# A list scheduler by highest level in place of one by program order, in a hybrid encoder block

## The reference

```python
h = rms_norm(x, norm_mix_g); proj = h @ w_in            # q 512, k 128, v 128, u 512
attn = window_attention(rope(q), rope(k), v, sink)      # 128-token blocks, +-128 window
ys = s5_bidirectional(u, ...)                           # 32 groups, complex state of 64,
                                                        # one scan in each direction
ys = gelu(ys); ys = ys * sigmoid(ys @ w_glu)
mixed = concat(rms_norm(attn), rms_norm(ys)); x = x + mixed @ w_out
h = rms_norm(x, norm_ffn_g)
up = depthwise_conv(h @ w_up, conv_w, conv_b)           # width 3, 2 x 2816 channels
x = x + (silu(up[gate]) * up[val]) @ w_down
return rms_norm(x, norm_final_g)
```

## Time and profile before

| | before |
|---|---|
| median of 3 runs | 1464.31 us (1461.26 to 1465.69) |
| profiled execution | 1461.61 us, span of the slowest core 1460.1 us |
| spans of the 8 cores | 1448.3 to 1460.1 us |
| PE, DVE, ACT busy | 1068.9, 989.2, 810.6 us |
| chain that ended last | PE 52%, DVE 17%, issue 12%, DMA 9%, ACT 8% |
| activation table loads | 20, of 1283 ns |

### The profile page before, as it was taken

How to read it: one execution, slowest core, us unless ns; L and a number is a source line. 1 busy time by engine, 2 the same in 40 slices (tenths; PEclk the granted TensorE clock), 3 DMA queues, 4 the chain that set the end, 5 groups by cost and what they waited for, 6 DMA issues and landing times.

```text
span 1460.1 us, 22892 instructions; the slowest of 8 cores (1448.3 to 1460.1 us)
## 1 busy us (share of the span) xinstructions
PE 1068.9 (73%) x6969; PEld 543.3 (37%) x6969; DVE 989.2 (68%) x1780; ACT 810.6 (56%) x1543; POOL 47.5 (3%) x63
## 2 busy tenths in 40 slices
PE   0159883686558577520887887599999999869996
PEld 0125441474323122110444444244544444424442
DVE  1576764848998999930677777388888888814322
ACT  2565562774333533252777776298888888723111
POOL 0001001010001000000000000000000000000000
PEclk9979987685555555555788888799999999979998
DMA  6743330000000000322122222522222221085331
GB/s 160 211 126 116 100 115 17 1 1 1 1 1 1 0 0 0 95 87 86 38 80 88 69 76 88 145 62 85 59 86 61 73 73 30 1 280 205 107 116 72
DMA packets 71320, 109.97 MB, mean 75 GB/s; under 512 B 4544, under 2 KB 50368, under 8 KB 71072
## 3 DMA queue, kind: packets, MB, share of 16 engines
q1 hardware_dynamic: 65344, 87.66, 20.7%
q0 software_dynamic: 5856, 20.85, 3.6%
HBM read 87.65 MB, written 20.85 MB: 74 GB/s over the span
## 4 chain that ended last, share of the span: by engine, by line
PE 52%; DVE 17%; issue 12%; DMA 9%; ACT 8%; SPq 1%; POOL 1%; DVEq 0%; ACTq 0%; POOLq 0%
PE ps L362 48%; DVE sb L342 11%; ACT sb L338 8%; PE ps L370 3%; DMA sb<-w_down 2%; DVE sb L787 2%; DVE sb L789 2%; DMA sb<-w_out 2%; DVE sb L354 1%; DMA sb<-x 1%; DVE sb L876 1%; DMA sb<-w_in 1%; PE ps L816 1%; DMA sb<-w_glu 1%; DMA sb<-w_up 1%
## 5 line engine op out<-in xcount | busy, mean ns | idle before, releaser
L362 PE MATMUL ps<-sb,sb 128*128 128x512 bf16 (+6 forms) x5089 | 779.6, 308 | 153.0 <-ACT sb L338 90.3
L362 PEld LDWEIGHTS ps<-sb,sb 128*128 128x128 bf16 (+1 forms) x5089 | 392.0, 101 | 535.5 <-issue 224.2
L338 ACT ACTIVATE sb<-sb 128x1 f32<-128x1 f32 (+11 forms) x589 | 340.4, 592 | 394.3 <-DVE sb L342 234.2
L338 ACT ACTIVATE sb<-ps 128x512 f32<-128x512 f32 (+7 forms) x666 | 323.0, 500 | 175.2 <-PE ps L362 142.7
L354 DVE SCALAR_TENSOR_TENSOR sb<-sb,sb,sb 128x1024 f32<-128x1024 f32 (+3 forms) x275 | 332.8, 1216 | 48.0 <-ACT sb L338 36.5
L342 DVE TENSOR_TENSOR sb<-sb,sb 128x272 f32<-128x272 bf16 (+10 forms) x572 | 287.7, 531 | 97.7 <-ACT sb L338 75.7
L342 DVE TENSOR_TENSOR sb<-ps,sb 128x512 f32<-128x512 f32 (+4 forms) x372 | 176.7, 498 | 103.4 <-PE ps L362 77.5
L769 PE MATMUL ps<-sb,sb 32*128 32x272 bf16 (+1 forms) x512 | 158.0, 509 | 72.2 <-DVE sb L342 72.2
L370 PE MATMUL ps<-sb,sb 128*128 128x128 bf16 x724 | 73.7, 269 | 100.6 <-DVE sb L342 55.3
L769 PEld LDWEIGHTS ps<-sb,sb 32*128 32x128 bf16 x512 | 64.4, 134 | 164.8 <-issue 146.8
L338 ACT ACTIVATE sb<-sb,sb,sb 128x1024 f32<-128x1024 f32 x88 | 109.2, 1241 | 5.1
(11 more groups left out here) (35 smaller groups left out, 154.2 us busy)
## 6 DMA issues: line engine op xcount, KB each, us to landing
sb<-x SPq DMA_DIRECT2D x49, 512.0 KB, 4.5
sb<-w_up SPq DMA_DIRECT2D x44, 512.0 KB, 3.9
sb<-w_down SPq DMA_DIRECT2D x22, 512.0 KB, 5.7
x_scr<-sb POOLq DMA_DIRECT2D x17, 512.0 KB, 5.1
sb<-x_scr SPq DMA_DIRECT2D x16, 512.0 KB, 3.7
y<-sb POOLq DMA_DIRECT2D x16, 512.0 KB, 2.9
sb<-w_in SPq DMA_DIRECT2D x8, 640.0 KB, 6.4
sb<-w_out SPq DMA_DIRECT2D x8, 512.0 KB, 3.8
```

What stands on the lines that cost most here:

```text
L338: return e.activation(out=out, in_=in_, func=func, scale=scale, **kw)
L362: ins = e.matmul(out, l, r, start=(i == 0), stop=(i == n - 1))
```

## The change

A second planner, `schedule_hlf`, is added and used (`KS_MODE` has 1 as its default; with 0 the old one is used). It first computes for each operation its level `bl`: its own planned cost and the largest level among its successors with a hop of 0.45 us, barriers included. Then it goes forward in time: of all engines it takes the one that can start something first; there, all operations that are ready by then are moved to a heap ordered by falling level (program order only breaks ties), and the highest is placed. Nothing else is changed: the operations, tiles, costs, predecessors and the way in which waits are written stay. Small differences: an operation without predecessors is ready at 0 instead of 0.45 us, and a barrier adds no hop of its own.

```diff
--- before.py
+++ after.py
@@ -159,9 +159,79 @@
         assert all(o.start is not None for o in ops), "scheduler: unscheduled ops (cycle?)"
         self.makespan = max(o.end for o in ops)
 
+    def schedule_hlf(self):
+        import heapq
+        ops = self.ops
+        succ = {id(o): [] for o in ops}
+        for o in ops:
+            for p in o.preds:
+                succ[id(p)].append(o)
+        bl = {}
+        for o in reversed(ops):
+            m = 0.0
+            for s_ in succ[id(o)]:
+                v = bl[id(s_)] + self.HOP
+                if v > m:
+                    m = v
+            bl[id(o)] = o.cost + m
+        npred = {id(o): len(o.preds) for o in ops}
+        eng_of = lambda o: self.streams[o.stream].eng_name
+        eng_free = {e: 0.0 for e in self.ENGS}
+        cand = {e: [] for e in self.ENGS}
+        avail = {e: [] for e in self.ENGS}
+
+        def rtime(o):
+            return (max(p.end for p in o.preds) + self.HOP) if o.preds else 0.0
+
+        def release(o):
+            for s_ in succ[id(o)]:
+                npred[id(s_)] -= 1
+                if npred[id(s_)] == 0:
+                    add(s_)
+
+        def add(o):
+            if o.stream is None:
+                o.start = o.end = max([p.end for p in o.preds], default=0.0)
+                release(o)
+            else:
+                heapq.heappush(cand[eng_of(o)], (rtime(o), o.prog, o))
+        for o in ops:
+            if npred[id(o)] == 0:
+                add(o)
+        left = sum(1 for o in ops if o.stream is not None)
+        while left:
+            best_e, best_t = None, None
+            for e in self.ENGS:
+                while cand[e] and cand[e][0][0] <= eng_free[e] + 1e-9:
+                    rt, pg, o = heapq.heappop(cand[e])
+                    heapq.heappush(avail[e], (-bl[id(o)], pg, o))
+                if avail[e]:
+                    t_ = eng_free[e]
+                elif cand[e]:
+                    t_ = max(eng_free[e], cand[e][0][0])
+                else:
+                    continue
+                if best_t is None or t_ < best_t:
+                    best_e, best_t = e, t_
+            e = best_e
+            if not avail[e]:
+                eng_free[e] = best_t
+                continue
+            _, pg, o = heapq.heappop(avail[e])
+            o.start = best_t
+            is_dma = self.streams[o.stream].inc == 16
+            o.end = best_t + o.cost
+            eng_free[e] = best_t + (0.08 if is_dma else o.cost)
+            left -= 1
+            release(o)
+        assert all(o.start is not None for o in ops)
+
     def emit(self, block):
         self.barrier()
-        self.schedule()
+        if _C("KS_MODE", 1) >= 1:
+            self.schedule_hlf()
+        else:
+            self.schedule()
         per_eng = {e: [] for e in self.ENGS}
         for o in self.ops:
             if o.stream is not None:
```

## The result

| | before | after |
|---|---|---|
| median | 1463.53 us (12 runs) | 1452.94 us (12 runs) |
| ratio | 1 | 0.9937, 95% interval 0.992 to 0.9953 |
| profiled execution | 1461.61 us | 1454.08 us |

Faster by 0.6%, where I had forecast 1.9% (1437 us). The sign and the range held, the size did not: of 27 us, about a third came.

What follows compares the result with a forecast made beforehand. No engine was taken as the bound everywhere; the limits differ by stage. Terms -11 - 3 - 2 - 4 - 7 + 0 = -27 us took the profiled 1461.6 to 1434.6, forecast as a 1437 us median, range 1410 to 1468.

Steps and rivals of the forecast that it cites:

- Boundaries (-11): Projection stage, six token-group boundaries: transposes move ahead of the last matmul groups, so PE waits less; -11 us.
- Rotary tables (-3): Projection stage: the cosine-table chain gets nearly the highest level, shortening PE's wait for the first rotation product; -3 us.
- Table build (-2): Table build stage: packing of the last powers moves ahead of copies that only end at the barrier; -2 us.
- Scan (-4): Scan stage: first scan input passes about two matmul groups, -2, and less is lost at the direction change, -2 us.
- At the turn: Scan stage, change of direction: cosine chain and scan products go ahead of the output table's memset-dependent operation; -2 us.
- Attention (-7): Attention stage: the next block's denominator and transposes pass the FFN-norm tail on DVE; -7 us.
- My second step: Attention: output matmuls and PSUM-freeing additions are late next, so only 1 of 3.7 us is gained in each of seven iterations.
- FFN (0): FFN stage: PE is contiguous, so no order can gain; 0 us, bounded by 0 and +33.
- the rival: FFN: interleaved gate and value finish in one DVE burst that starves PE; +33 us, 1470 us; chance 0.18.
- Down projection (0 to +3): Down projection: PE contiguous, its start a load paced by DMA, not by order; 0 to +3 us.
- more table loads: First stage: ten further ACT table loads on the path cost 13 us, giving 1450 us; chance 0.08.
- full gains: Rotary stall mostly gone (-13) and attention gives 20, sum -50, giving 1414 us; chance 0.12.

Runs made afterwards that it cites:

- pe_only: The new planner with levels deciding on TensorE alone, in all stages, and program order on every other engine; 1451.26 us.
- ssq_cost: New planner, levels on TensorE alone in stage 1, all engines in 3 and 4; sum of squares planned at 1.25 us, not 0.5; 1438.21 us.
- edges: New planner, levels in stages 1, 3 and 5 only, one-column edge matmuls raised 20 us in stage 5, memset planned at 6.9 us; stage 5 349.0 us.
- best: New planner, levels on TensorE in stage 1, all engines in 3 and 4; true memset and sum-of-squares costs, measured costs in stage 4; 1421.76 us, ratio 0.972.
- hop4: As best, but in stage 4 the planned hop is 0.15 us for 0.45 and the planned durations stay mostly old; stage 4 294.2 us.

## Why the prediction was right or wrong

**Boundaries (-11): right in the mechanism, in the size partly by luck.** Stage 1 gave -10.5: transposes stand among matmuls, and PE's waits are down from 13.0 to 4.4 us, 8.6 less (I had named under 3 us as the sign). The rest comes from a term that I had put at nothing: PE's own busy time behind the rotary wait falls by 4.2 us for the same matmuls, at a granted clock of 0.96 for 0.93. pe_only shows that it is TensorE's order. The levels of the other engines add nothing: 215.1 without them against 219.7, or 216.4 to 216.7 where the same order ran again, so that what they cost, if anything, is not settled.

**Rotary tables (-3): nothing came.** The wait was 6.29 us after, 5.25 before. The order did not help: the first product depends on all five blocks. I had this dependence in the text and still gave the order 3 us; changing it gives 8.7.

**Table build (-2): +0.5**, within what the cores differ by.

**Scan (-4): -7.8, and the reason given is wrong.** "So matmul groups can swap only within about six places" is false: each tile of the ring is a lane of its own, in which groups keep their order, and one lane can run far ahead of the others. The first scan matmuls passed 14 groups, not two, and started 19.7 us into the stage, not 32. But that is not where the gain comes from either: pe_only has them as early and gains 1.7 us, the other engines' levels alone give 4.4, and only both together 7.8. Which operations on DVE and ACT do it was not tried, so that the total came near is luck. At the turn the matmuls went forward as forecast and the memset did not: the plan believes that it takes 0.5 us. Its true cost adds 4 us (320.4 against 324.3). The 0.82 us between the two scans of the earlier trace rows comes from a dependence that the program records and the data do not have: neither scan reads the other's result, their outputs only share one name. By those spacings it costs about 0.2 us in each of 32 pairs, an estimate that no run tried.

**Attention (-7): -0.2, the step that failed most.** "The new order lets those pass" assumes that the tail and the next block's denominator stand ready together in the plan. They hardly ever do: of DVE's 321 operations in this stage the plan of after places 16 while another one is ready (9 in before's). I had not looked at what the plan believes. Its blocks are 17.3 to 18.2 us apart, and of that PE has 15.7, ACT 13.4 and DVE 11.5; the chip takes 13.6 in after, with PE busy 184.18/17 = 10.8. With PE and the hops taken for so long, DVE waits, and takes each operation as it comes. The tail stayed on the chain, in nine blocks where before had seven.

That is half of the answer. With the measured costs the planned blocks are 12.5 us apart, 63 of the 321 are placed from a choice, the stage is 12 us shorter, and still the rule is worth nothing clear: 285.6 by program order, 281.7 to 284.2 by levels. So it is not that levels pick better once there is something to pick; the costs change the planned starts, and that helps under either rule. My second step failed as well: in ssq_cost the tail leaves the chain in nearly all blocks and the time stays, as what is late next is as late. How much of the 12 to 14 us is a higher granted clock, and why ACT's and DVE's true durations harm alone and help together with TensorE's, stays open.

**FFN (0): +6.3, a part of the rival.** Its first half was right: gate and value are interleaved, the edges come last, and edges brings 5 of the 6.3 back. Its price was not: "If 1.5 us of the 2.6 us of delay reaches PE in each pair" gives 33 us, but PE has one gap of 0.82 us in 22 pairs. The burst of 5.07 us does not reach PE in the other pairs, which fits the six PSUM tiles and the separate tiles for the two halves that I had named; behind the last pair the barrier waits for it: 3.9 us. Why PE's matmuls themselves take 1.6 us more is not shown. "PE is contiguous, so no order can gain" holds; that an order can lose at the stage's end was missing.

**Down projection (0 to +3): +2.6**, against a spread of 4 us between cores. The same order ran in pe_only and gave +0.7, so no loss by the order is shown.

**The sum.** The measured differences by stage add to -9.1, the forecast's to -27. The largest errors are attention (6.8 us), the FFN (6.3), stage 1 (3.5), the down projection (2.6) and the table build (2.5), less 3.8 that the scan gave beyond its term. The rivals of more table loads (20 in both profiles) and of full gains did not come.

## What to carry to other kernels

A list scheduler's rule decides only between operations that the plan holds ready together; before changing the rule, compare its planned length of a stage and busy time of each engine with the trace, and mend the durations that are far off (6.92 us planned as 0.5 gave 4 to 5 us here, TensorE's 15.7 for 10.8 gave 7.6). Mend them stage by stage: the same true costs made three other stages longer. Take the rule stage by stage and engine by engine, since barriers make the stages add: best was forecast at a ratio of 0.972 from the parts and measured 0.972. Read TensorE's busy time and granted clock beside a stage's time: the same matmuls took 166 to 194 us in stage 4 here. A level that ends at a barrier knows nothing of cheap, late inputs such as one-column edges, and a dependence drawn too wide cannot be scheduled away.

## What the runs showed of the hardware

The granted clock moved with the order of the same matmuls, and not simply with the span. By core it was 0.807 to 0.814 before, 0.808 to 0.815 after and 0.820 to 0.828 in best, whose slowest core is 31 us shorter than after's; but 0.802 to 0.810 in hop4, whose slowest core is 21 us shorter. Most of that is stage 4, where the medians go from 0.72 to 0.80 and PE's busy time from 193.7 to 177.0 us.

In after the 16 scan matmuls of 512 columns at the turn took 7.00 us, 0.44 each, in a stage whose granted clock was 0.56, near the lower level of 1.2 GHz (512/1.2 = 427 ns); TensorE had been waiting 3.66 us for DVE shortly before.

Two SCALAR_TENSOR_TENSOR of 128x1024 f32 on DVE start 1.38 us apart in before's pair at 1269.75, where the second needs the first's result, and 1.20 us apart in the middle of after's burst at 1259.94, where they belong to different convolutions. That fits DVE's 7.6 us less of busy time in stage 5; DVE was not what bounded the stage.
